# Transposes of attention probabilities moved between the halves of a slot's stream matmuls, and one panel of q transposed a slot later

## The reference

```python
z  = rmsnorm(x, norm1) @ w_in                       # split into eleven parts
xr = rg_lru(causal_conv(z_rx), ...)                 # recurrent mixer
y_a = (xr * gelu(z_ry)) @ w_rg_out
q  = rmsnorm(z_q.reshape(B, S, 16, 64), q_norm)
kc = rmsnorm(compress(z_kc), k_norm[0]); vc = compress(z_vc)
k_s, k_w = rmsnorm(z_ks, k_norm[1]), rmsnorm(z_kw, k_norm[2])
y_b = nsa(q, kc, vc, k_s, v_s, k_w, v_w, sigmoid(z_ng)) @ w_nsa_out
x  = x + (sigmoid(z_mg0) * y_a + sigmoid(z_mg1) * y_b) @ w_o
x  = x + (silu(h2 @ w_gate) * (h2 @ w_up)) @ w_down   # h2 = rmsnorm(x, norm2)
```

## Time and profile before

| | |
|---|---|
| device time, median of 3 runs | 537.23 us (536.66 to 537.76) |
| span of the profiled execution | 535.1 us |
| what lies around the span, against the median | 2.1 us |
| PE busy | 515.7 us (96%) |
| VectorE (DVE) busy | 317.4 us (59%) |
| ScalarE (ACT) busy | 283.0 us (53%) |
| POOL busy | 56.2 us (10%) |
| mean granted TensorE clock | 0.981 of full speed |

### The profile page before, as it was taken

The page is one execution under the profiler, slowest core; times in us unless marked ns, Lnnn a source line. Parts: engine busy times, 40 slices in busy tenths (PEclk is TensorE's granted clock), DMA queues, the critical chain, the costliest instruction groups (busy, mean ns, idle before and its releaser), DMA issues.

```text
span 535.1 us, 8092 instructions
## 1 busy us (share of the span) xinstructions
PE 515.7 (96%) x3235; PEld 458.3 (86%) x3235; DVE 317.4 (59%) x418; ACT 283.0 (53%) x431; POOL 56.2 (10%) x93
## 2 busy tenths in 40 slices
PE   6999999699999889999999999799999999999997
PEld 6998998588989667777777788699999999988886
DVE  3999798799654654536464375654455455453432
ACT  5655978776357677564745343643533543543320
POOL 1000200940111322121211000000000000000000
PEclk9999999899799999999999999799999999999999
DMA  8645464625242224333623445064544555555502
GB/s 341 238 159 172 145 230 163 232 86 232 80 158 80 79 80 157 110 127 90 225 85 152 158 157 216 20 237 165 211 176 165 204 182 168 199 186 170 223 0 78
DMA packets 12546, 84.76 MB, mean 158 GB/s; under 512 B 1504, under 2 KB 1504, under 8 KB 2656
## 3 DMA queue, kind: packets, MB, share of 16 engines
q1 hardware_dynamic: 11808, 82.32, 42.3%
q0 software_dynamic: 272, 1.05, 0.6%
q10 hardware_dynamic: 432, 0.91, 0.4%
HBM read 83.22 MB, written 1.05 MB: 157 GB/s over the span
## 4 chain that ended last, share of the span: by engine, by line
PE 79%; issue 8%; ACT 4%; POOL 4%; DVE 3%; DMA 1%; POOLq 0%; DVEq 0%
PE bank L1035 23%; PE bank L1037 22%; PE bank L1036 22%; PE bank L1168 3%; PE bank L1132 2%; PE bank L1143 2%; POOL rs L311 2%; PE bank L1172 1%; PE bank L1170 1%; POOL pbuf L337 1%; DMA xs<-x_dram 1%; POOL scr L323 1%; ACT pbuf L428 1%; DVE w_lo L646 1%; PE bank L1133 1%
## 5 line engine op out<-in xcount | busy, mean ns | idle before, releaser
L646 DVE TENSOR_TENSOR w_lo<-raw,w_hi 128x2048 fp32r<-128x2048 f32 x77 | 179.2, 2331 | 125.7 <-ACT w_hi L359 125.3
L359 ACT ACTIVATE w_hi<-raw 128x2048 fp32r<-128x2048 f32 x77 | 147.3, 1918 | 116.5 <-PE bank L1037 115.7
L1035 PE MATMUL bank<-h_hi,w_hi 128*128 128x256 f32 x512 | 147.3, 288 | 1.0 <-DVE h_lo L693 1.0
L1036 PE MATMUL bank<-h_lo,w_hi 128*128 128x256 f32 x512 | 146.4, 286 | 0.0
L1037 PE MATMUL bank<-h_hi,w_lo 128*128 128x256 f32 x512 | 146.3, 286 | 0.0
L1035 PEld LDWEIGHTS bank<-h_hi,w_hi 128*128 128x128 f32 x512 | 99.9, 195 | 1.8 <-issue 1.6
L1036 PEld LDWEIGHTS bank<-h_lo,w_hi 128*128 128x128 f32 x512 | 99.9, 195 | 0.0
L1037 PEld LDWEIGHTS bank<-h_hi,w_lo 128*128 128x128 f32 x512 | 99.8, 195 | 0.0
L1035 PE MATMUL bank<-w_hi,act 128*128 128x512 f32 (+1 forms) x184 | 69.1, 376 | 0.0
L1037 PE MATMUL bank<-w_hi,act 128*128 128x512 f32 (+1 forms) x184 | 68.4, 372 | 0.0
L1036 PE MATMUL bank<-w_lo,act 128*128 128x512 f32 (+1 forms) x184 | 68.3, 371 | 0.0
(11 more groups left out here) (203 smaller groups left out, 551.0 us busy)
## 6 DMA issues: line engine op xcount, KB each, us to landing
raw<-stream_dram SPq DMA_DIRECT2D x77, 1024.0 KB, 4.8
xs<-x_dram POOLq DMA_DIRECT2D x1, 1024.0 KB, 5.5
out_dram<-xs SPq DMA_DIRECT2D x4, 256.0 KB, 2.0
xs<-x_dram ACTq DMA_DIRECT2D x1, 512.0 KB, 5.0
xs<-x_dram SPq DMA_DIRECT2D x1, 512.0 KB, 4.8
scr<-small_dram ACTq DMA_DIRECT2D x1, 320.0 KB, 10.2
prm<-params_dram ACTq DMA_DIRECT2D x1, 58.0 KB, 7.4
```

The lines of the kernel that those rows point to most:

```text
L359: sc.activation(w_hi[:, i % HL, :], raw[:, i % RAW, :], ACT.Copy).then_inc(hi_ready, 1)
L646: ve.tensor_tensor(w_lo[:, i % HL, :], raw[:, i % RAW, :], f(w_hi[:, i % HL, :]), ALU.subtract).then_inc(lo_ready, 1)
L1035: pe.matmul(out_, l_hi, r_hi, start=start, stop=False)
L1036: pe.matmul(out_, l_hi, r_lo, start=False, stop=False)
```

## The change

PE transposes panel qa after slot 15 instead of slot 14, and ScalarE and VectorE read it in slot 16 instead of 15. The bank order of the small units is adapted (`kcn` before `qTa`). In the slots of the heads PE begins with the scores; both turns of the previous head stand between the halves of the stream matmuls, behind the compressed transposes in slot 21. In every slot after 20 that is not in `SPLIT_LAST`, ScalarE splits first of all, and VectorE splits after the maxima. The order of ScalarE's other work (L404, L410, L412, L418, L428) is unchanged.

```diff
-MISC_ORDER = [..., ("hidk", 1), ("qTa", 2), ("kcn", 1), ("kcT", 1),
+MISC_ORDER = [..., ("hidk", 1), ("kcn", 1), ("qTa", 2), ("kcT", 1),
...
             for i in range(NSLOT + 2):                      # ScalarE
                 h = i - HEAD0
+                ahead = i not in SPLIT_LAST and i > HEAD0
+                if ahead:
+                    split_hi(i + AHEAD)
...
-                if i not in SPLIT_LAST:
+                if i not in SPLIT_LAST and not ahead:
                     split_hi(i + AHEAD)
...
-                    if i == FIRST[name] + 5:
+                    if i == FIRST[name] + (6, 5)[pnl]:
...
                     ve.tensor_scalar(ast[:, 1, :], ...).then_inc(max_ready, 1)   # VectorE
+                ahead = i not in SPLIT_LAST and i > HEAD0
+                if ahead:
+                    split_lo(i + AHEAD)
...
             for i in range(NSLOT):                          # TensorE
                 h = i - HEAD0
-                if 1 <= h <= HEADS:
-                    turn_a(h - 1)
                 if 0 <= h < HEADS:
                     scores(h)
-                if 1 <= h <= HEADS:
-                    turn_b(h - 1)
+
+                def turns():
+                    if h == 1:
+                        compressed_transposed()
+                    if 1 <= h <= HEADS:
+                        turn_a(h - 1)
+                        turn_b(h - 1)
...
-                        direct(i, ..., units,
-                               compressed_transposed if i == HEAD0 + 1 else None)
+                        direct(i, ..., units, turns)
...
-                        panel(i, r % 2, ..., h_of(h_hi), h_of(h_lo))
+                        panel(i, r % 2, ..., h_of(h_hi), h_of(h_lo), None, turns)
...
-                        between = (lambda: merged_transposed(0)) if (name, r) == ("nso", 3) else None
+                        between = (lambda: merged_transposed(0)) if (name, r) == ("nso", 3) else turns
...
-                    if i == FIRST[name] + 4:
+                    if i == FIRST[name] + (5, 4)[pnl]:
                         pe.wait_ge(qn_ready, 2 * pnl + 2)
```

More of the change, by code:

```diff
@@ L58 @@
 USE_RY = [USE["ry0"]] + [USE["ry1"] + _n for _n in range(3)]
-MISC_ORDER = [("xT", 4), ("ng", 1), ("ngT", 1), ("kT", 4), ("hidk", 1), ("qTa", 2), ("kcn", 1), ("kcT", 1),
+MISC_ORDER = [("xT", 4), ("ng", 1), ("ngT", 1), ("kT", 4), ("hidk", 1), ("kcn", 1), ("qTa", 2), ("kcT", 1),
               ("qTb", 2), ("hidv", 1), ("cmps", 2), ("vrep", 1), ("att", 4 * HEADS), ("mT", 4), ("hT2", 4)]
@@ L1187, in _ @@
                         units = {FIRST["rx"]: MISC["xT"], FIRST["gu"]: MISC["hT2"]}.get(i)
-                        direct(i, USE_RY[r] if name == "ry" else USE[name] + r, h_hi, h_lo, units,
-                               compressed_transposed if i == HEAD0 + 1 else None)
+                        direct(i, USE_RY[r] if name == "ry" else USE[name] + r, h_hi, h_lo, units, turns)
                 for name in ("kk", "vv", "qa", "qb", "mg"):
@@ L1192, in _ @@
                     if 0 <= r < dict(ORDER)[name]:
-                        panel(i, r % 2, USE[name] + r // 2 * 2, h_of(h_hi), h_of(h_lo))
+                        panel(i, r % 2, USE[name] + r // 2 * 2, h_of(h_hi), h_of(h_lo), None, turns)
                 for name in ("rgo", "nso", "wo"):
```

## The result

The changed kernel takes 543.6 us (median of 4 runs, 543.5 to 545.6) against 536.9 for the kernel before in the same runs (4, 534.8 to 537.8): a ratio of 1.0135, 95% interval 1.0103 to 1.0167, so 6.7 us more. The prediction of 540.1 had the sign right and the size less than half; 543.6 also lies above its range. The profiled span is 542.7 us against 535.1, 7.6 more; the profiled execution is the longest of the four (545.6, the others 543.5 to 543.7). The first row of the page answers to the earlier trace rows: PE is as busy a share as before, with the same 3235 matmuls.

A forecast was written before the change was run, and what follows sets the result against it. PE, busy 96% of the span, was taken to bound the kernel. The terms +1.4 + 0 + 0 + 0.85 + 0.7 = +2.95, taken as +2.9, gave 540.1 us; forecast's own range 539.0 to 541.5, 8-in-10 range 536.0 to 542.6.

The forecast's parts named there:

- part 1: Transposes of qa a slot later: the wait for POOL goes, but VectorE delivers piece 18 late, +1.4 us, bounds -0.9 to +4.8.
- the 11.83 us of VectorE: VectorE's sequence from the start of the scan until piece 18 is ready for PE, including L863 of qa: 11.83 us.
- The same course: Before slot 17: clock falls 2.0 us after PE stops and stays low 6.84 us, covered by the wait for piece 18.
- My upper bound for part 1: Late scan with the clock also falling behind slot 18: +1.4 + 3.4 = +4.8 us.
- Part 2: Turns between the stream halves in the head slots: 0 for the move, 0 in slot 21, +0.85 and +0.7 in slots 24 and 26.
- Slots 24 and 26: POOL waits of 1.50 and 1.78 us go; waits for exponentials and y_lo replace them, 2.35 and 2.45: +0.85 and +0.7.
- the bounds of -0.06 to +0.13: Cost per head slot of moving the turns in itself; over 16 slots -1.0 to +2.1 us, taken as 0.
- The rival of a clock fall in slot 24 (0.15): Clock also falls in one of the gelu slots 24 and 26: 1.7 to 3.4 us more, 541.8 to 543.5, chance 0.15.
- Part 3: Splits first in ScalarE's slots: they already hide behind the matmuls and hold nothing up, 0 us.
- The reading of L933: L933 took 2.07 us against 1.36 for two halves; the extra 0.7 was read as waiting for POOL's L323 until 98.44.
- plain gain: Rival: PE's idle times go and nothing replaces them, 526.8 us, half of it 532; chance 0.12 for all gains over 1.1 us.
- The clock stays up: Rival: the scan starts at once and the 4.1 us idle before slot 18 don't lower the clock, +0.65, 537.9; chance 0.18.

The follow-up runs named there:

- this part alone: Kernel before with only the transposes of panel qa, and their readers, moved a slot later: 541.47 us, ratio 1.0092 to the kernel before.
- the changed kernel's second profile: The changed kernel run once more with no edit: 544.30 us, ratio 1.0127 to the kernel before.
- the heads' part alone: Kernel before with only the turns between the stream halves and the splits first, qa's transposes at their old place: 539.60 us, ratio 1.0059.
- the experiment that held the product: Changed kernel with POOL's second product L329 held until VectorE's first four scans are done: 541.41 us, ratio 1.0083 to the kernel before.
- its three edits: Changed kernel with POOL's second product held, second scans in slot 19 and gelu ahead of the turns' copies: 535.44 us, ratio 0.9974.
- two of them: Kernel before with the gelu first in slots 23 and 25 and the second scans in slot 19: 533.15 us, ratio 0.9917.

## Why the prediction was wrong

**The step that failed** is the end of part 1: "piece 18 at 108.7 + 11.83 = 120.5. Against 119.16 that is +1.4". Slot 18 did start at 120.41, and what leads there held to within 0.15 us: the scan at work from 108.7 behind L329, the 11.83 us of VectorE, piece 17 at 113.36. But I took that lateness for the price of the part, as though PE bounded all that follows. It is +4.8 with this part alone (interval 3.4 to 6.4). Behind piece 18, VectorE and POOL were late too. The new place of L863 had pushed the sums of qb and with them POOL's powers by 2.0 us; the one that VectorE waits for took another 2.0 us more; and VectorE's queue (L810, scan, L869, L900) had no slack until 134.46. I followed the late engine to PE's next wait and not to the point where it had slack again. What the runs showed in place of the missing 3.4 us: 1.27 us of waiting for L900 and 1.7 us of longer slow clock in one profile, 3.15 us of slow clock in slot 18 in the other.

**The clock** was right for the stretch I followed and wrong as a rule. "The same course" of 2.0 us and 6.84 us was read off two stretches; the traces have 3.41, 6.83 and 10.25, and the same kernel has it covered in slot 17 in one execution and again in slot 18 in the next. I had left out the fall behind the compressed scores, which the kernel before had as well and which the change made longer in one of its two profiles. My upper bound for part 1, +4.8 from a fall behind slot 18, is the course of the changed kernel's second profile; I gave it a place in the range's reasoning but no rival and no chance of its own, though the sum with it (4.8 + 1.55 = 6.35, 543.6 us by the prediction's own working) is the time measured. That the number agrees so well is luck in part: the first profile came to it by another way, the low stretch in slot 17 covered as forecast and the loss further on.

**Part 2** held step by step. Slot 21's wait: 0.55 us for 0.65. Slots 24 and 26: scores waiting 0.50 and 0.29, stream matmuls 1.00, together +0.9 and +0.7 for +0.85 and +0.7; the probabilities' scaling by POOL never waited for. The 0.08 us per quiet slot lay inside the bounds of -0.06 to +0.13 and was taken as 0: over ten slots 0.8 us, and the heads' part alone is +2.9 (interval 2.0 to 4.3) where 1.55 was forecast. That it comes from the second restart of the stream is argued only. The rival of a clock fall in slot 24 (0.15) is seen in the first profile of the change, and neither in its second nor in that of the heads' part alone.

**Part 3** held. The reading of L933 was looser than it was put: 0.7 us more than two short ones reach from 97.45 to 98.15, not to the 98.44 at which L323 ends. It pointed the right way; what shows that the scan waits for POOL's product is the experiment that held the product. The *plain gain* fell, for the reason given against it. *The clock stays up* fell at its first condition: the scan didn't start at once. Held apart, by the experiment on POOL's product, the early scan did bring the pieces at 111.1 and 118.2, and the clock did fall.

**Left open**: how the timed 4.8 us of the panel's part divide between wait and clock, since the executions differ in just that. Whether the clock stays up when PE's idle time is filled with other work wasn't tried. Open too are the 2.3 us that separate the changed kernel with its three edits from the kernel before with two of them.

## What to carry to other kernels

When a step moves, follow the engine that becomes late (here VectorE, with the POOL operations that it feeds) until its timeline shows idle time again; PE's next wait is only the first bill, and here it was a quarter of the sum. When a wait for engine B is at the end of a chain through engine A, look first whether A stood idle ahead of its own part: moving the gelu of two slots on an idle ScalarE gave 3.0 us, where moving PE's turns gave new waits in the same slots. Treat each idle gap of PE of a few microseconds as carrying a slow-clock bill whose place one profile does not fix: bound it by the longest stretch seen, all of it at work, and give that case a chance. And when mends make a change break even, apply them to the kernel before as well: here that kernel was then 2.3 us faster.

## What the hardware showed that I had not expected

- The contention of VectorE and POOL goes both ways: a scan of 0.66 us took 2.80 behind a POOL product, and a POOL product of 2.39 took 4.46 behind a split (and a small power of 128x8 took 1.64 us alone, 3.62 in the kernel before and 5.66 in the changed one, beside the same two splits, which start at 116.81 and 118.09). L869, with one input from PSUM, took 3.06 in either place. The Trainium skill's page "SBUF — State Buffer", section "Who interferes with whom", has the one issued first hold the port; the scan and the product agree, the power of 5.66 us doesn't. It ends 1.64 us, its length alone, after 123.02, so by this estimate it was kept out by three VectorE instructions in a row (two splits and L810), the last two of them issued after it. What decides when POOL gets in between is open.
- The slow clock came in stretches of 3.41, 6.83 and 10.25 us, and in the kernel before it fell at 135.97, although the timeline has no wait of PE's between 103.88 and there, behind the matmuls of 32 and 64 columns at the end of slot 19.
- A summed 1.8 us of idle time in three pieces, with matmuls between, was followed by a fall of the clock in slot 24 in two of the six profiles that have these three waits there, and in only one of the two executions of the changed kernel.
